# Issuing the two DMA transposes of q and k back to back on the sync queue of a hybrid attention decoder layer

## The chip, the cores and the metric

The kernel runs on 1 core of one Trainium2 chip. The metric is the time of one execution on the device in microseconds (us), the median of several runs. The engines are named as in the profile: PE is TensorE, DVE is VectorE, ACT is ScalarE, POOL is GpSimd, and SP is SyncE, whose queue (SPq) issues nearly all the DMAs.

## The reference

One decoder layer on 256 tokens of width 2048, in float32:

```
h    = rmsnorm(x) ; proj = h @ w_in               # 2048 -> 8192 columns
dq, dk, dv, mq, mk, mv, gate = split(proj)        # 8 "diff" heads, 8 "moba" heads, 128 wide
d_out: per head two softmaxes over 64-wide halves of q and k (causal, ALiBi),
       attn = p0 - lambda * p1 ; rmsnorm(attn @ v) * (1 - 0.2)
m_out: per head causal softmax with ALiBi (with 256 tokens the only block is the own one)
x    = x + (concat(d_out, m_out) * silu(gate)) @ w_out
x    = x + cross attention of rmsnorm(x) (4 heads) into rmsnorm(mem), projected by w_o_mem
out  = rmsnorm(x)
```

## The kernel before

Every float32 matmul with a weight is made of three matmuls on fp32r values: a weight tile w is split into w_hi (an ACT copy, L819) and w_lo = w - w_hi (a DVE subtraction, L1057), the activations likewise, and PE adds hi\*hi, hi\*lo and lo\*hi (L560 to L562). A "half" is 2 x 128 rows by 512 columns of weights, and PE spends 12 matmuls on it. The loads of the raw halves go into a ring of eight buffers (`w_raw`), the split halves into rings of four.

The input projection is cut into 8 pairs of heads, each with 16 halves: halves 0 to 7 make q and k of the pair, halves 8 to 15 make v and gate. The code calls the 16 halves of one pair a window. Pairs 0 to 3 are diff heads, pairs 4 to 7 moba heads. In the window of pair j each engine walks n = 0 to 15, first its share of the splitting for half n + 2 (ACT, DVE) or the matmuls of half n (PE), and then the pieces of attention that are due at n. PE's window j holds the values part of pair j - 1 and the scores of pair j. Since "the pair before" of windows 1 to 4 is a diff pair, those four windows hold the longer chain for y.

The path of q and k of pair a, inside window a:

- n = 8, ACT L847: two copies take q and k (token tiles t = 0 and t = 1) out of PSUM and write them as two planes of 16-bit halves, into `qk_planes` (in the memory of `mems`).
- SP L404 to L409, `turn_qk(a, t)`: waits for the copy of tile t and issues a DMA transpose of 128 x 1024 16-bit values into `qkT_planes`. The profile shows it as DMA_TRANSPOSE at L408.
- POOL L513 to L521, `merge_qk`: for each t it waits until the transpose has landed, and copies the planes back together into `qkT_sb` (L518; in the profile `pool<-mems`).
- n = 12: ACT L852 makes qT_hi and L854 the high part of k; DVE L1103 scales k, and L1109 makes the two low parts.
- n = 13: PE L609 to L617, the scores, which wait for the low parts (`qkT_ready`).

The path of y of the pair before (windows 1 to 4), in the same window: DVE at n = 9, behind the splitting of half 11, runs a chain of fifteen tiny instructions on 128 x 4 values (L1160 to L1171, a reciprocal square root by Newton steps, each waiting for the one before); at n = 10, behind the splitting of half 12, it makes y (L1182 x4). ACT at n = 11 copies y to planes (L896), then splits half 14 (L819), and only then comes to L852. DVE splits half 14 and then comes to L1103. POOL merges the transposed y at L528.

SP's own loop is written by halves too: `load_pair_half` waits until the half that lay in the ring buffer eight halves earlier has been split (`lo_made`) and issues two loads of 256 KB. So SP works on the loads of window j while the other engines are at about n = 8 of window j - 1, and `turns(n, j)` puts the transposes of pair j - 1 behind the loads of half n. All of SP's DMAs leave it in the order of the program. The tail (L451 to L459) does the same for the last pair.

Of the kernel before, what the change touches and what calls it, by code (L numbers as in the profile page):

```python
# [33 lines left out]
NT = SEQ // P  # L34
# [59 lines left out]
X_PARTS = ((0, 256), (256, 512), (512, 1024), (1024, 1536), (1536, 2048))  # L94
WARM_UP = (5, 4, 2)

QK_TURN_AT = (1, 2)
Y_TURN_AT = 4
P_TURN_AT = (10, 11)
MEM_LOAD_AT = 14  # L100
# [26 lines left out]
def program(nc, x, mem, norm_mix_g, w_in, lambda_q1, lambda_k1, lambda_q2, lambda_k2,  # L127
            subln_g, w_out, norm_mem_g, mem_norm_g, w_q_mem, w_kv_mem, w_o_mem, final_g, out):
    with ExitStack() as ctx:
# [249 lines left out]
        def _(sp):  # L379
# [17 lines left out]
            def turn_probabilities(a, u):  # L397

                sp.wait_ge(planes_ready, 2 * a + u + 1)
                sp.nop(nofuse=True)  # L400
                sp.dma_start_transpose(probT_planes[:, u].rearrange("p (i q) -> p i q", q=P), prob_planes[:, u]
                                       ).then_inc(planes_turned[u], 16)

            def turn_qk(a, t):  # L404

                sp.wait_ge(qk_planes_ready, 2 * a + t + 1)
                sp.nop(nofuse=True)
                sp.dma_start_transpose(qkT_planes[:, t].rearrange("p (i q) -> p i q", q=P), qk_planes[:, t]  # L408
                                       ).then_inc(qk_turned[t], 16)  # L409

            def turn_y(a):

                sp.wait_ge(y_planes_ready, a + 1)
                sp.nop(nofuse=True)
                sp.dma_start_transpose(yT_planes.rearrange("p t c -> p (t c)").rearrange("p (i q) -> p i q", q=P),
                                       y_planes.rearrange("p t c -> p (t c)")).then_inc(y_turned, 16)

            def turns(n, j, y_too=True):

                if n in QK_TURN_AT:  # L420
                    turn_qk(j - 1, n - QK_TURN_AT[0])
                if n == Y_TURN_AT and y_too:
                    turn_y(j - 2)
                if n in P_TURN_AT:
                    turn_probabilities(j - 1, n - P_TURN_AT[0])
# [14 lines left out]
            for n in range(PAIR_HALVES):  # L440
                load_pair_half(DIFF, 1, 1, n)
                turns(n, 1, False)
            with sp.Fori(2, KIND_PAIRS) as j:
                for n in range(PAIR_HALVES):
                    load_pair_half(DIFF, j, j, n)
                    turns(n, j)
            with sp.Fori(KIND_PAIRS, PAIRS) as j:
                for n in range(PAIR_HALVES):
                    load_pair_half(MOBA, j, j - KIND_PAIRS, n)
                    turns(n, j)  # L450
# [955 lines left out]
```

## Time and profile before

| | us |
|---|---|
| median of 3 runs | 589.99 (589.55 to 590.5) |
| the profiled execution, its own time | 590.55 |
| its span, first to last instruction | 588.4 |

| engine | busy us | share of the span |
|---|---|---|
| PE (matmuls) | 574.3 | 98% |
| DVE | 434.6 | 74% |
| ACT | 338.5 | 58% |
| POOL | 75.5 | 13% |

The mean granted clock of TensorE is 0.994 of its 2.4 GHz level. 16 DMA engines were busy for 66.4% of the span with SP's queue. A row of a timeline gives the start and the length of an instruction or of a run of them (x2 is two in a row), and in brackets how long its engine sat idle before it and what ended that. A row of the waits gives an engine and line, who it waited for, the sum in us, the number of times and the longest.

### The profile page before, as it was taken

Reading aid. Unit: us, or ns where it says so; the run is one execution under the profiler, and the core shown is the slowest. Engines: PE = TensorE matmul, PEld = TensorE weight load, DVE = VectorE, ACT = ScalarE, POOL = GpSimd, SP = SyncE. Lnnn points to the kernel's source line nnn. Section 1 sums busy time; section 2 is a strip of 40 time slices with the busy share of each in tenths; the row PEclk is TensorE's granted clock in tenths of the full one; section 3 lists DMA queues with packets and bytes.
Section 4 is the critical chain, followed back from the end, with each engine's and each line's share of the span. In section 5 each row is a group of like instructions: output and inputs, shape, how many; then the busy total and the mean of one; then the engine's idle time right before and its main releaser. Section 6 shows DMA issues by size and latency. Waiting matters only on the chain.

```text
span 588.4 us, 8726 instructions
## 1 busy us (share of the span) xinstructions
PE 574.3 (98%) x2738; PEld 479.1 (81%) x2738; DVE 434.6 (74%) x693; ACT 338.5 (58%) x564; POOL 75.5 (13%) x87
## 2 busy tenths in 40 slices
PE   8999999999999999999999999999999999999994
PEld 7878887887888788788888888888888888888883
DVE  4688769888987988886866866957576656755875
ACT  5765754864664774665664664673466665445723
POOL 2010202203111211221310420310000000000000
PEclk9999999999999999999999999999999999999997
DMA  8996766777577677787776874978555555554303
GB/s 276 317 311 215 207 181 180 208 210 202 175 227 188 202 217 188 223 240 194 217 225 168 241 221 146 265 206 320 180 177 155 186 187 189 176 184 144 107 1 143
DMA packets 128349, 117.68 MB, mean 200 GB/s; under 512 B 44050, under 2 KB 110147, under 8 KB 127811
## 3 DMA queue, kind: packets, MB, share of 16 engines
q1 hardware_dynamic: 128290, 117.36, 66.4%
q8 instruction: 13, 0.21, 0.1%
q14 instruction: 14, 0.11, 0.1%
q10 hardware_dynamic: 32, 0.01, 0.0%
HBM read 106.06 MB, written 2.10 MB: 184 GB/s over the span
## 4 chain that ended last, share of the span: by engine, by line
PE 85%; DVE 6%; issue 4%; ACT 4%; ACTq 0%; POOL 0%; DVEq 0%; POOLq 0%
PE ps L560 24%; PE ps L562 24%; PE ps L561 24%; PE ps L591 2%; PE ps L627 2%; ACT w_hi L819 2%; PE ps L609 1%; PE ps L783 1%; PE ps L788 1%; PE ps L784 1%; PE ps L570 1%; DVE pool L1182 1%; DVE w_lo L1057 1%; DVE kT_parts L1109 1%; ACT mems L847 1%
## 5 line engine op out<-in xcount | busy, mean ns | idle before, releaser
L1057 DVE TENSOR_TENSOR w_lo<-w_raw,w_hi 128x1024 fp32r<-128x1024 f32 x187 | 242.6, 1300 | 102.6 <-ACT w_hi L819 100.3
L819 ACT ACTIVATE w_hi<-w_raw 128x1024 fp32r<-128x1024 f32 x187 | 196.1, 1059 | 111.5 <-PE ps L562 109.3
L560 PE MATMUL ps<-w_hi,aT 128*128 128x512 f32 x576 | 226.7, 394 | 0.0
L562 PE MATMUL ps<-w_hi,aT 128*128 128x512 f32 x576 | 224.3, 389 | 0.0
L561 PE MATMUL ps<-w_lo,aT 128*128 128x512 f32 x576 | 224.3, 389 | 0.0
L562 PEld LDWEIGHTS ps<-w_hi,aT 128*128 128x128 f32 x576 | 108.1, 188 | 22.8
L560 PEld LDWEIGHTS ps<-w_hi,aT 128*128 128x128 f32 x576 | 108.2, 188 | 22.5 <-issue 0.4
L561 PEld LDWEIGHTS ps<-w_lo,aT 128*128 128x128 f32 x576 | 108.2, 188 | 21.6
L560 PE MATMUL ps<-w_hi,yT_hi 128*128 128x512 f32 x128 | 50.5, 395 | 0.0
L562 PE MATMUL ps<-w_hi,yT_lo 128*128 128x512 f32 x128 | 49.9, 390 | 0.0
L561 PE MATMUL ps<-w_lo,yT_hi 128*128 128x512 f32 x128 | 49.8, 389 | 0.0
L518 POOL COPY pool<-mems 128x1024 uint16<-128x1024 uint16 x16 | 24.2, 1514 | 166.8 <-DMA mems<-mems 166.8
L864 ACT ACTIVATE pool<-pool,small 128x256 f32<-128x256 f32 (+1 forms) x48 | 21.3, 446 | 21.3 <-DVE small L1129 21.3
L1094 DVE RECIPROCAL pool<-pool 128x128 f32<-128x128 f32 x32 | 30.5, 953 | 1.1
L562 PEld LDWEIGHTS ps<-w_hi,yT_lo 128*128 128x128 f32 x128 | 24.0, 188 | 5.0
L561 PEld LDWEIGHTS ps<-w_lo,yT_hi 128*128 128x128 f32 x128 | 24.1, 188 | 4.8
L560 PEld LDWEIGHTS ps<-w_hi,yT_hi 128*128 128x128 f32 x128 | 24.0, 188 | 4.7
L847 ACT ACTIVATE mems<-ps 128x1024 uint16<-128x1024 uint16 x16 | 15.5, 1020 | 18.5 <-PE ps L562 18.5
L509 POOL COPY probT<-mems 128x768 uint16<-128x768 uint16 x16 | 18.2, 1140 | 59.8 <-DMA mems<-mems 59.8
L1067 DVE SCALAR_TENSOR_TENSOR aT<-ps,gainsT,aT 128x256 fp32r<-128x256 f32 x32 | 14.0, 478 | 13.5 <-ACT aT L829 13.5
L502 POOL TENSOR_TENSOR alibi<-dist,slopes 128x256 f32<-128x256 f32 x16 | 15.5, 987 | 58.6 <-DVE small L1129 58.5
L829 ACT ACTIVATE aT<-ps,gainsT 128x256 fp32r<-128x256 f32 x32 | 13.4, 473 | 14.1 <-PE ps L591 14.1
(166 smaller groups left out, 537.4 us busy)
## 6 DMA issues: line engine op xcount, KB each, us to landing
w_raw<-in_w_in SPq DMA_DIRECT2D x256, 256.0 KB, 3.1
w_raw<-in_w_out SPq DMA_DIRECT2D x64, 256.0 KB, 3.6
w_raw<-in_w_kv_mem SPq DMA_DIRECT2D x32, 256.0 KB, 2.9
w_raw<-in_w_q_mem SPq DMA_DIRECT2D x16, 256.0 KB, 2.9
w_raw<-in_w_o_mem SPq DMA_DIRECT2D x16, 256.0 KB, 3.4
mems<-in_mem SPq DMA_DIRECT2D x1, 2048.0 KB, 9.7
xs<-in_x SPq DMA_DIRECT2D x3, 512.0 KB, 8.3
w_raw<-in_final_g SPq DMA_DIRECT2D x1, 1024.0 KB, 4.6
```

The source lines that it names most:

```text
L502: pool_e.tensor_tensor(alibi[:, u], dist[:, :], slope, ALU.mult).then_inc(alibi_ready, 1)
L509: pool_e.tensor_copy(probT[:, u].rearrange("p i q -> p (i q)").bitcast(U16) .rearrange("p (c h) -> p h c", h=2), probT_planes[:, u].rearra ...
L518: pool_e.tensor_copy(qkT_sb[:, :, t * P:(t + 1) * P].bitcast(U16) .rearrange("p i (q h) -> p h i q", h=2), qkT_planes[:, t].rearrange("p ( ...
L560: pe.matmul(acc, hi[:, k0 + k, tok], w_hi[:, slot, k], start=first and k == 0, stop=False)
L561: pe.matmul(acc, hi[:, k0 + k, tok], w_lo[:, slot, k], start=False, stop=False)
L562: m = pe.matmul(acc, lo[:, k0 + k, tok], w_hi[:, slot, k], start=False, stop=last and k == GK // 2 - 1)
L819: act.activation(w_hi[:, i % SPLITS], raw, ACT.Copy).then_inc(hi_made, 1)
L847: act.activation(qk_planes[:, t].rearrange("p (h c) -> p h c", h=2), ps[:, t, :].bitcast(U16).rearrange("p (c h) -> p h c", h=2), ACT.Copy ...
L864: m = act.activation(prob_sb[:, u, c, cols], prob_sb[:, u, c, cols], ACT.Exp, bias=neg_max[:, u, t, c:c + 1], accum_out=exp_sum[:, c, u, t ...
L1057: dve.tensor_tensor(lo, w_raw[:, i % RAW], hi.bitcast(F32), ALU.subtract).then_inc(lo_made, 1)
L1067: m = dve.scalar_tensor_tensor(lo, ps[:, bank + i, (k % 2) * SEQ:(k % 2 + 1) * SEQ], gainsT[:, gain:gain + 1], hi.bitcast(F32), ALU.mult, ...
L1094: dve.reciprocal(s, s).then_inc(silu_steps, 1)
```

## The change

`QK_TURN_AT` was the pair (1, 2): the transpose of token tile 0 was issued behind the loads of half 1, that of tile 1 behind the loads of half 2. Now both are issued behind the loads of half 1, tile 0 first, and the loads of half 2 follow them. The same holds for the loop of window 1, for the two loops over j and for the tail. No other engine's program is touched, and no instruction is added or removed.

```diff
-QK_TURN_AT = (1, 2)
+QK_TURN_AT = 1
 ...
             def turns(n, j, y_too=True):
 
-                if n in QK_TURN_AT:
-                    turn_qk(j - 1, n - QK_TURN_AT[0])
+                if n == QK_TURN_AT:
+                    for t in range(NT):
+                        turn_qk(j - 1, t)
```

## Rows read from the trace of the kernel before

**Rows 1.** The page, part 1: busy us, share of the span, instructions.
```profile
PE 574.3 (98%) x2738; PEld 479.1 (81%) x2738; DVE 434.6 (74%) x693; ACT 338.5 (58%) x564; POOL 75.5 (13%) x87
```
**Rows 2.** The waits of the whole run: sum us, times, longest.
```profile
ACT qT_hi L852 <- POOL pool L518: 1.6, 4, 0.6
PE ps L609 <- DVE kT_parts L1109: 3.1, 4, 0.8
```
**Rows 3.** ACT's splitting by line: busy, mean ns, then idle before and releasers.
```profile
L819 ACT ACTIVATE w_hi<-w_raw 128x1024 fp32r<-128x1024 f32 x187 | 196.1, 1059 | 111.5 <-PE ps L562 109.3 <-DMA w_raw<-in_w_in 2.0
```
**Rows 4.** The waits of ACT within the first 33 us.
```profile
ACT w_hi L819 <- DMA w_raw<-in_w_in: 2.0, 2, 1.6
```
**Rows 5.** Timeline of window 2, SP's queue: start, length, instruction.
```profile
129.62 1.26 SPq L408 DMA_TRANSPOSE mems<-mems  x1
131.14 0.94 SPq L389 DMA_DIRECT2D w_raw<-in_w_in  x2
132.25 1.23 SPq L408 DMA_TRANSPOSE mems<-mems  x1
133.72 6.31 SPq L389 DMA_DIRECT2D w_raw<-in_w_in  x4
```
**Rows 6.** Timeline of window 2, ACT.
```profile
128.53 1.94 ACT L847 ACTIVATE mems<-ps 128x1024 uint16<-128x1024 uint16 x2 [1.99 <-PE ps L562]
...
140.01 1.06 ACT L896 ACTIVATE mems<-pool 128x1024 uint16<-128x1024 uint16 x1 [4.99 <-DVE pool L1182]
...
141.93 0.62 ACT L852 ACTIVATE qT_hi<-pool 128x512 fp32r<-128x512 f32 x1
```
**Rows 7.** Timeline of window 2, POOL: the two merges of q and k.
```profile
132.83 1.34 POOL L518 COPY pool<-mems 128x1024 uint16<-128x1024 uint16 x1 [14.45 <-DMA mems<-mems]
136.58 1.35 POOL L518 COPY pool<-mems 128x1024 uint16<-128x1024 uint16 x1 [2.41 <-DMA mems<-mems]
```
**Rows 8.** Timeline of window 2, DVE: parts of the Newton chain, splitting, y, k.
```profile
132.99 1.14 DVE L1164 SCALAR_TENSOR_TENSOR small<-small 128x4 f32<-128x4 f32 x1
134.16 0.17 DVE L1167 TENSOR_SCALAR small<-small 128x4 f32<-128x4 f32 x1
134.37 0.17 DVE L1076 TENSOR_SCALAR small<-small 128x4 int32<-128x4 int32 x1
134.57 0.16 DVE L1080 SCALAR_TENSOR_TENSOR small<-small 128x4 f32<-128x4 f32 x1
...
136.63 2.31 DVE L1057 TENSOR_TENSOR w_lo<-w_raw,w_hi 128x1024 fp32r<-128x1024 f32 x1
138.87 1.11 DVE L1182 SCALAR_TENSOR_TENSOR pool<-ps,small,pool 128x128 f32<-128x128 f32 x4
...
144.59 1.01 DVE L1109 TENSOR_TENSOR kT_parts<-pool,kT_parts 128x512 fp32r<-128x512 f32 x1
```
**Rows 9.** Timeline of PE: the scores of window 2, and of window 5.
```profile
145.65 0.50 PE L609 MATMUL ps<-kT_parts,qT_hi 64*128 64x256 f32 x4 [0.81 <-DVE kT_parts L1109]
...
286.49 0.40 PE L609 MATMUL ps<-kT_parts,qT_hi 128*128 128x256 f32 x2
```
**Rows 10.** Line L1057 over the run: min/median/max ns, first and last start.
```profile
L1057 DVE TENSOR_TENSOR w_lo<-w_raw,w_hi x187: 1206/1225/2315, 9.9 to 560.1; 128x1024 fp32r<-128x1024 f32 x187
```
**Rows 11.** Timeline of DVE: the splitting of half 12 in windows 1, 3, 4.
```profile
89.44 2.14 DVE L1057 TENSOR_TENSOR w_lo<-w_raw,w_hi 128x1024 fp32r<-128x1024 f32 x1
...
184.16 2.17 DVE L1057 TENSOR_TENSOR w_lo<-w_raw,w_hi 128x1024 fp32r<-128x1024 f32 x1
...
231.26 2.20 DVE L1057 TENSOR_TENSOR w_lo<-w_raw,w_hi 128x1024 fp32r<-128x1024 f32 x1
```
**Rows 12.** Line L1164 over the run: min/median/max ns.
```profile
L1164 DVE SCALAR_TENSOR_TENSOR small<-small x4: 161/1136/1153, 85.8 to 227.7; 128x4 f32<-128x4 f32 x4
```
**Rows 13.** Timeline of POOL near 257 us: a merge of probabilities.
```profile
256.60 2.05 POOL L509 COPY probT<-mems 128x768 uint16<-128x768 uint16 x1 [1.82 <-DMA mems<-mems]
```
**Rows 14.** Timeline of DVE near 257 us: a tensor_scalar twice.
```profile
257.65 1.08 DVE L1092 TENSOR_SCALAR pool<-pool 128x128 f32<-128x128 f32 x1
...
261.10 0.22 DVE L1092 TENSOR_SCALAR pool<-pool 128x128 f32<-128x128 f32 x1
```

## The prediction

> **What bounds the kernel now.** I read the page first. PE is busy for 574.3 of 588.4 us [rows 1], so whatever an edit of the DMA order does, it can only change PE's idle time, 14 us in all, most of it at the two ends. Next I read the waits, for the places where the path of q and k could hold PE up. There is one: PE stands at L609 for 3.1 us in four windows [rows 2]. These are windows 1 to 4; the one of window 2 is 0.81 us [rows 9]. In window 5 PE comes to the same line with no idle time [rows 9]. So a reader's question is what ends last in front of L609 in windows 1 to 4, and the timelines of one such window on SP, ACT, POOL and DVE answer it.
>
> In window 2 ACT finishes the two planes of q and k at 130.47 [rows 6], SP issues the turns at 129.62 and 132.25 with two loads between them [rows 5], and POOL merges them at 132.83 to 134.17 and 136.58 to 137.93 [rows 7]. The merged q and k are read by ACT L852 only at 141.93 [rows 6]: the second merge is 4.0 us early. L852 is late for another reason: ACT sat idle for 4.99 us before L896 [rows 6], waiting for DVE's y (L1182, 138.87 to 139.98) [rows 8]; then come L896, one splitting and L852, each right behind the other. DVE's k part ends at 145.60 [rows 8], PE starts at 145.65 [rows 9]. The last thing in front of L609 is therefore the chain Newton steps, splitting of half 12, y, L896, L852, k. A microsecond more or less in that chain is one in PE's wait, as long as 0.8 us are not used up.
>
> Then I compared POOL's and DVE's rows, since these touch that chain. L1164 works on 4 elements per partition, and takes 1.14 us while POOL's first merge runs; it ends at 134.13, POOL at 134.17 [rows 7, 8]. Its neighbours of the same size take 0.16 to 0.17 [rows 8]. The splitting of half 12 begins 0.05 us after the second merge and takes 2.31 us against a median of 1.225 [rows 7, 8, 10]. So each merge stops the DVE instruction that starts behind it until the copy is over, and both stops lie in the chain that PE waits for. This pattern stands in all four windows: 2.14, 2.17 and 2.20 in the other three [rows 11]; L1164 has it in three of them, with a median of 1.136 [rows 12], and in the fourth it is the instruction ahead of it.
>
> **The change part by part.** It removes nothing and adds nothing; it moves one transpose per pair ahead of two loads.
>
> *The loads of half 2* go from 131.14 to about 1.49 us later (a turn of 1.23 and the gap of 0.26 that stands between 130.88 and 131.14) [rows 5], and the loads of half 3 then start at 133.6 to 133.7, where they start now. Each load fills a buffer that is used eight halves later, some 21 us. ACT waited for a load for 2.0 us in the whole run [rows 3], all of it in the first 33 us [rows 4], ahead of the first moved turn. Cost nothing; the cover is some 15 us deep.
>
> *The wait of the second turn* now stands ahead of the loads of half 2. It is for the second plane, ready at 130.47, before the first turn has left SP at 130.88 [rows 5, 6]. Cost nothing.
>
> *The second merge.* A turn takes 3.21 us from issue to the start of its merge (129.62 to 132.83), and the second, behind 512 KB of loads, 4.33 (132.25 to 136.58) [rows 5, 7]. The trace shows no two turns back to back. By the first row it lands at 131.14 + 3.21 = 134.35; by the other at 135.5. I take 134.35, since then too nothing stands between it and an idle queue but a turn that has already been sent. The merge starts 0.18 us behind the end of the first instead of 2.41 us.
>
> This earlier merge gains nothing on the path of q and k, by the 4.0 us above. In windows 5 to 7 and 0 ACT does wait for it, 1.6 us in all [rows 2], but PE has no idle time there [rows 9]. Worth nothing.
>
> *What the merge stops on DVE.* Removed: the stop of the splitting of half 12, 2.14 + 2.31 + 2.17 + 2.20 - 4 x 1.225 = 3.92 us over four windows. Added: a copy of 1.35 us that starts at 134.35, in the middle of the Newton chain, which now runs undisturbed from 134.16 to 136.5. Which step it stops isn't shown for this size. If a tensor_scalar is stopped too, it is L1076 at 134.37 [rows 8]: it ends at about 134.35 + 1.35 - 0.04 = 135.66 instead of 134.54, 1.12 us. If only the instructions with two inputs are stopped, it is L1080 at 134.57, ending at 135.66 instead of 134.73, 0.93 us, and up to 0.2 less in a window where two tensor_scalars are still ahead. The four windows run in nearly the same phase, so the sums are 4.48 and 3.5 to 3.7. The nearest row for a tensor_scalar is L1092 at 257.65, 1.08 us instead of 0.22 while a POOL copy ran to 258.65 [rows 13, 14]; it is wider (128 instead of 4), but the same operation. I take the first: 4.48 - 3.92 = +0.56 us; the other end is -0.3.
>
> What the rows show here has a rule: the Trainium skill, SBUF — State Buffer, section "Who interferes with whom", says that DVE and GpSimd share a pair of ports as an exclusive lock, held for the whole instruction, that DVE instructions with two SBUF inputs contend with a GpSimd instruction that reads SBUF, and that a tensor_scalar can when it runs in a two-port mode. L1164 (two inputs, 1.14) and L1092 (1.08) agree. By that rule the time would be the +0.56 of the sum if the 4-wide steps run in such a mode, and -0.3 if they don't; no row here shows which.
>
> *The end of window and the rest.* Behind the chain everything (L896, turn of y, L852, k) keeps its distances. The profiled execution would go from a span of 588.4 to about 589.0. Its own time was 590.55, 0.56 above the median of the three runs, so I add the difference to the median: 589.99 + 0.56 = 590.5.
>
> **The rivals.**
>
> 1. *Only two-input steps are stopped*: the same story with the other end of the price, -0.3, 589.7. For it: it needs no assumption about 4-wide tensor_scalars; against it: L1092.
> 2. *The second turn lands as late as it does now*, or somewhere in the chain's second half, for instance since two transposes are served one after the other. Then the stop falls on another step of the same chain, or again on the splitting: 590.0 to 590.4. For it: no row shows two turns in a row. Against it: nothing much.
> 3. *Slower: POOL doesn't give the port back between the merges.* The second copy needs only to have landed within the first, that is 1.34 us after it instead of my 1.52. SP's spacing could be 1.26 plus a gap of 0.1 rather than 0.26 [rows 5]. If POOL then goes first, L1164 waits for two copies. Each window loses 1.35 + some 0.1 and gets back 0.98 (3.92 / 4): +0.47, four times, +1.9 us, 591.9. Against it: in the rows DVE's stopped instruction ended 0.04 us before POOL's record, so it seems to be the next in line; and my estimate leaves 0.18 us.
> 4. *Faster: the merge is what L609 waits for after all.* Then up to the whole 3.1 us [rows 2] come back, 586.9. Against it the 4.0 us between the merge and L852 [rows 6, 7].
>
> **How the numbers follow.** Forecast 590.5: 0.42; rival 1, 0.28; rival 2, 0.18; rival 3, 0.09; rival 4, 0.03. The runs before spread over 0.95 us, so about 0.2% (1.2 us, that is 588.8 and 591.2) is what a measurement can tell from no change. Forecast and rivals 1 and 2 lie inside it; a little of each leaks over the edge by scatter. Faster 0.05, same 0.84, slower 0.11. The range goes from rival 1 less 0.6 of scatter to just under rival 3: 589.1 to 591.6.
>
> **What would show it right or wrong.** In the profile after: the turns of a pair 1.5 us apart on SP and the loads of half 2 behind them; the second merge 1.5 us behind the first instead of 3.75; the splitting of half 12 back at 1.2 us in windows 1 to 4; in its place a second step of the Newton chain at 1.1 to 1.3 us, a tensor_scalar (L1167 or L1076) for the forecast, L1080 to L1084 for rival 1; ACT no longer waiting for POOL at L852; PE's wait at L609 still in four windows with 3.5 us instead of 3.1 (2.8 for rival 1, 4.9 for rival 3, none for rival 4). Everything else within 0.1 us. I would be wrong if ACT began to wait for loads, if the turns slowed each other beyond 136.6, or if the moved merge met an instruction in windows 5 to 7 that PE waits for.

## The result: 0.22% slower, with both of VectorE's stops now in the Newton chain

| | before | after |
|---|---|---|
| median of 20 runs, same job | 589.83 | 591.10 |
| lowest and highest | 588.49, 591.11 | 590.90, 591.58 |
| ratio, 95% interval | | 1.0022, 1.0015 to 1.0029 |
| the profiled execution, its own time | 590.55 | 591.33 |
| its span | 588.4 | 589.2 |

All times are in us. A job is a set of runs made together. The time went up by 1.27 at the median, but only by 0.78 between the two profiled executions. In the changed kernel the lines of the file from L421 on are one higher: L1057 of before is L1058 of after, L1076 is L1077, L1167 is L1168.

The first thing to look at is window 2 again. On SP's queue the two turns are now in a row, and six loads follow, where rows 5 had turn, loads, turn, loads:

```profile
130.07 2.69 SPq L408 DMA_TRANSPOSE mems<-mems  x2
133.00 7.66 SPq L389 DMA_DIRECT2D w_raw<-in_w_in  x6
```

POOL's two merges (rows 7: 132.83 and 136.58) are in a row too, 2.68 us for two copies of 1.34:

```profile
133.54 2.68 POOL L519 COPY pool<-mems 128x1024 uint16<-128x1024 uint16 x2 [14.69 <-DMA mems<-mems]
```

And this is DVE's timeline across them (answering rows 8), from the Newton chain to y:

```profile
133.44 0.16 DVE L1165 SCALAR_TENSOR_TENSOR small<-small 128x4 f32<-128x4 f32 x1
133.63 1.29 DVE L1168 TENSOR_SCALAR small<-small 128x4 f32<-128x4 f32 x1
134.96 1.29 DVE L1077 TENSOR_SCALAR small<-small 128x4 int32<-128x4 int32 x1
136.28 0.16 DVE L1081 SCALAR_TENSOR_TENSOR small<-small 128x4 f32<-128x4 f32 x1
...
138.34 1.23 DVE L1058 TENSOR_TENSOR w_lo<-w_raw,w_hi 128x1024 fp32r<-128x1024 f32 x1
139.48 1.12 DVE L1183 SCALAR_TENSOR_TENSOR pool<-ps,small,pool 128x128 f32<-128x128 f32 x4
```

Two tensor_scalars of 4 elements per partition, 0.17 us each when nothing else runs (rows 8), take 1.29 us each, one per copy. The splitting of half 12 is back from 2.31 to 1.23 us. So each window has two stopped DVE instructions, as before; one of the two has moved from the splitting into the Newton chain. PE's wait at the scores (rows 9: 0.81) is

```profile
146.27 0.51 PE L610 MATMUL ps<-kT_parts,qT_hi 64*128 64x256 f32 x4 [0.91 <-DVE kT_parts L1110]
```

and over the run (rows 2), with ACT's waits for loads (rows 3, 4) and for the merge:

```profile
PE ps L610 <- DVE kT_parts L1110: 3.6, 4, 0.9
ACT w_hi L820 <- DMA w_raw<-in_w_in: 1.7, 2, 1.5
ACT qT_hi L853 <- POOL pool L519: 1.0, 1, 1.0
```

So PE waits 3.6 us instead of 3.1, in the same four windows. The two tensor_scalars repeat in each of them: L1168 takes 1.21 to 1.29 us, L1077 1.24 to 1.33. ACT waits no more for loads than it did, and for the merge once, in window 0, where PE has no idle time. The scores of window 4 begin 0.76 us later than in the profile of before, those of window 7 0.80, and the span is 0.8 longer: 0.11 of it was there at the scores of window 0 already, and 0.65 arises from there to the scores of window 4.

### The profile page after: what moved, and what is told of

It reads as the page before. It is cut to its first block, busy times and chain, and to the rows that moved or that the text cites. A ratio compares the mean times of both kernels' runs of the same rounds, so it can differ in the third digit from the quotient of the medians.

```text
span 589.2 us, 8726 instructions
## 1 busy us (share of the span) xinstructions
PE 574.2 (97%) x2738; PEld 478.4 (81%) x2738; DVE 432.9 (73%) x693; ACT 338.7 (57%) x564; POOL 76.7 (13%) x87
## 4 chain that ended last, share of the span: by engine, by line
PE 81%; DVE 7%; issue 4%; ACT 3%; SPq 3%; DMA 2%; ACTq 0%; DVEq 0%
PE ps L561 24%; PE ps L563 23%; PE ps L562 23%; PE ps L628 2%; ACT w_hi L820 2%; DMA w_raw<-in_w_in 2%; SPq L389 1%; PE ps L610 1%; PE ps L785 1%; PE ps L784 1%; PE ps L789 1%; PE ps L592 1%; DVE small L1077 1%; DVE small L1168 1%; DVE pool L1183 1%
## 5 line engine op out<-in xcount | busy, mean ns | idle before, releaser
L1058 DVE TENSOR_TENSOR w_lo<-w_raw,w_hi 128x1024 fp32r<-128x1024 f32 x187 | 235.4, 1262 | 105.1 <-ACT w_hi L820 103.1
L519 POOL COPY pool<-mems 128x1024 uint16<-128x1024 uint16 x16 | 28.0, 1779 | 152.0 <-DMA mems<-mems 152.0
```

The lines of the kernel that those rows point to most:

```text
L519: pool_e.tensor_copy(qkT_sb[:, :, t * P:(t + 1) * P].bitcast(U16) .rearrange("p i (q h) -> p h i q", h=2), qkT_planes[:, t].rearrange("p ( ...
L1058: dve.tensor_tensor(lo, w_raw[:, i % RAW], hi.bitcast(F32), ALU.subtract).then_inc(lo_made, 1)
```

## The experiments

The theory: each POOL merge stops one DVE instruction for the length of the copy; if that instruction is in the chain to y, PE pays. The rivals: that the order on the DMA queue costs something itself, and that an early merge is what counts. A second question was why the medians differ by more than the profiles.

### Both kernels once more (e1, e2)

No edit. 

> The kernel before, unchanged, timed and profiled once more. Theory (race): in the first profile the second merge of q and k on POOL started within 0.25 us of the DVE's splitting of half 12 in each of windows 1 to 4, and DVE was stopped four times out of four; whoever is first holds the port. In another execution DVE should be first in some windows: the splitting then takes 1.2 us instead of 2.1 to 2.3, the copy is stopped instead, and PE's wait at the scores of that window falls from 0.8 to 0 to 0.2 us. Expected here: median 589.8, runs spread over 2 us, at least one window of the profile won by DVE. Rival (the spread has nothing to do with the merges): all four windows as in the first profile, whatever the time of the execution.

> The changed kernel, unchanged. Theory (race): both copies start in the middle of the Newton chain, where DVE is always stopped twice, so there is nothing left to win: median 591.1, spread below 0.7 us, and the profile again shows L1168 and L1077 at 1.2 to 1.3 us in all four windows. Rival: the spread is as wide as that of the kernel before.

On this chip the 23 runs of the kernel before that stand beside e1 to e4 took 590.53 (588.65 to 590.93); e1, 12 more runs of the same kernel, took 590.29 (588.73 to 590.75), ratio 0.9996 (0.9987 to 1.0005). The changed kernel took 591.04 (590.90 to 591.61), ratio 1.0013 (1.0005 to 1.0022). The half of the expectation about the spread holds: 0.7 us against over 2. The race did not show: the profile of e1 (590.18) has four stops in four windows. But it showed that the second merge isn't tied to its place. It starts 3.20 to 3.88 us behind the first, and in windows 1 and 4 it stopped a step at the end of the Newton chain (L1084, 1.18 us, and L1171, 1.23 us) instead of the splitting. In e2 L1168 and L1077 take 1.21 to 1.33 us in all four windows, as expected.

### The second merge held back until y is made (e3, e4)

```diff
                 for t in range(NT):
+                    if t == 1 and not isinstance(a, int):
+                        pool_e.wait_ge(y_ready, a)
                     pool_e.wait_ge(qk_turned[t], 16 * a + 16)
```

e3 has this in the kernel before, e4 in the changed one.

> The order of turns of the kernel before; the second merge of q and k on POOL waits in addition until DVE has made y of that window (y_ready), from pair 1 on. Theory (the port stop in the chain of y is the whole price): the splitting of half 12 takes 1.2 us always, y comes 1.0 us earlier, PE's wait at the scores falls from 0.8 to under 0.2 us in windows 1 to 4, and the time is 587.3 to 588.0. Rival (the merge is needed early by ACT or PE): ACT waits for the late merge, PE's wait stays or grows, 590 or more.

> The order of turns of the changed kernel, with the same gate as the run before. Theory (the moved loads and the two turns in a row cost nothing, only the place of the second copy does): the same time as with the order of before, within 0.3 us, 587.3 to 588.0. Rival (the order on the DMA queue has a cost of its own, from the loads of half 2 that come later or from turns that slow each other): about 1.3 us slower than the gated kernel with the order of before.

Measured: 586.91 (ratio 0.9946, 0.9934 to 0.9958) and 587.00 (0.9947, 0.9935 to 0.9959). That is 0.3 to 0.4 us below the lower end of what the theory expected, and the two are equal within 0.1. With the gate the second merge has the same place in both, and the first still stops one step of the Newton chain in each, so the two kernels differ in the order on the DMA queue and in little else, and no difference is left to see. The rival of the queue, which had 1.3 us, falls. In window 2 of e3 the splitting of half 12 is free, and the merge is the one that is stopped, 2.19 us, while DVE splits half 13:

```profile
138.17 2.19 POOL L520 COPY pool<-mems 128x1024 uint16<-128x1024 uint16 x1 [4.89 <-DVE pool L1184]
```
```profile
135.75 1.23 DVE L1059 TENSOR_TENSOR w_lo<-w_raw,w_hi 128x1024 fp32r<-128x1024 f32 x1
136.90 1.12 DVE L1184 SCALAR_TENSOR_TENSOR pool<-ps,small,pool 128x128 f32<-128x128 f32 x4
137.94 1.21 DVE L1059 TENSOR_TENSOR w_lo<-w_raw,w_hi 128x1024 fp32r<-128x1024 f32 x1
```

PE's row of waits at the scores is gone from e3 and e4 altogether. From the scores of window 2 to those of window 3 PE is now busy for all of 46.45 us, where it had been 46.59 busy and 0.80 idle. So a window gives back its wait and some 0.1 us of recorded matmul time besides, which is how 3.1 us of waits became 3.6 of time, and PE leaves nothing more to win there.

### The opposite of the change (e5)

```diff
-QK_TURN_AT = (1, 2)
+QK_TURN_AT = (1, 3)
 ...
-                    turn_qk(j - 1, n - QK_TURN_AT[0])
+                    turn_qk(j - 1, QK_TURN_AT.index(n))
```

> The opposite of the change: the second turn goes behind the loads of half 3 instead of half 2. No wait is added. Theory (the place of the second copy is all that counts): SP issues it some 1.5 us later than before, it lands at about the start of y or behind it, the splitting of half 12 is not stopped, PE's waits of windows 1 to 4 are gone, and the time is that of the gated kernels, 586.8 to 587.6, with a spread below 0.7 us. Rival (the earlier the transposes are, the better; or it was the gate itself that helped): 590 or more.

586.82 (586.81 to 587.22), ratio 0.9947 (0.9933 to 0.9960). With no wait added, a turn issued later gives 3.4 us, about as much as the gate. In window 2 the second merge starts at 138.21, behind y, and it is now late for ACT, which waits 0.34 us for it at L852 there, 10.7 us in six windows over the run. PE doesn't notice:

```profile
138.21 2.10 POOL L518 COPY pool<-mems 128x1024 uint16<-128x1024 uint16 x1 [4.98 <-DMA mems<-mems]
```
```profile
ACT qT_hi L852 <- POOL pool L518: 10.7, 6, 2.6
```

This answers "the earlier the better": here the merge is later, ACT waits over six times as long as in the kernel before (1.6, rows 2), and the kernel is faster by 0.5%. It also shows that a stop costs by its place. In windows 1 and 3 POOL was first again, and the splitting of half 13, behind y, was stopped. Two splittings take 3.39 us here, with one stopped, and PE had no wait in these windows either:

```profile
91.11 1.37 POOL L518 COPY pool<-mems 128x1024 uint16<-128x1024 uint16 x1 [4.33 <-DMA mems<-mems]
```
```profile
91.42 3.39 DVE L1057 TENSOR_TENSOR w_lo<-w_raw,w_hi 128x1024 fp32r<-128x1024 f32 x2
```

### A third copy behind the two (e6)

```diff
                                        ).then_inc(qk_merged, 1)
+                pool_e.tensor_copy(spare.rearrange("p (r c) -> p r c", r=2),
+                                   dist[:, :].bitcast(U16).unsqueeze(1).to_broadcast([P, 2, 2 * SEQ]))
```

> The changed kernel with a third copy on POOL behind the second merge of each pair, of 1024 16-bit values from dist into a tile that nobody reads (extra work; the result is the reference's). Theory (each POOL copy behind the other stops one more instruction of the Newton chain for its whole length, and PE waits for the chain): L1081 or its neighbour takes 1.1 to 1.3 us as well, PE's waits grow by 1.1 to 1.2 us in each of four windows, 591.1 + 4.4 to 4.9 = 595.5 to 596.0. Rival (what matters is when the merge is ready, or DVE loses only the first stop): 591.1 to 592, since nobody waits for the third copy.

594.15 (594.09 to 594.50), 3.05 above the 591.10 that the changed kernel took in the job of the result, where 4.4 to 4.9 were expected. The mechanism is as expected, and the size is off since this copy is shorter. POOL and DVE in window 2:

```profile
134.37 2.73 POOL L520 COPY pool<-mems 128x1024 uint16<-128x1024 uint16 x2 [14.73 <-DMA mems<-mems]
137.00 1.04 POOL L524 COPY spare<-dist 128x1024 uint16<-128x1024 uint16 x1
```
```profile
134.38 1.29 DVE L1168 SCALAR_TENSOR_TENSOR small<-small 128x4 f32<-128x4 f32 x1
135.70 0.17 DVE L1171 TENSOR_SCALAR small<-small 128x4 f32<-128x4 f32 x1
135.91 1.21 DVE L1080 TENSOR_SCALAR small<-small 128x4 int32<-128x4 int32 x1
137.15 0.91 DVE L1084 SCALAR_TENSOR_TENSOR small<-small 128x4 f32<-128x4 f32 x1
```

A copy of 1.04 us stops L1084 for 0.91 - 0.16 = 0.75 us. The other three windows have 0.75, 0.75 and 0.74 at the same line, together 3.0, and 3.05 were measured. Nobody waits for this copy; it costs only by what it stops. PE's wait at the scores is 3.6, as in the changed kernel, and a second one has come up, since half 12 is split too late for its matmuls:

```profile
PE ps L564 <- DVE w_lo L1061: 1.9, 4, 0.5
```

That is 1.9 of the 3 us. Most of the rest lies in PE's busy time, which is 0.16 to 0.28 us higher from one window's scores to the next than in the changed kernel (46.79 against 46.51 in the last of them).

### Both merges held back (e7)

The same gate for both token tiles (`if not isinstance(a, int):`), in the kernel before.

> The order of turns of the kernel before, and both merges of q and k on POOL wait until DVE has made y. Theory (PE's waits in windows 1 to 4 were all that there was to win, and one stop less wins them whole): the Newton chain is not stopped at all and y comes another 1.0 us earlier, but PE has nothing left to wait for, so 586.9 again, within 0.3 us; or up to 1 us more if the two merges, now in a row behind y, hold L852 up. Rival (each stop has its price, 0.8 to 1 us per window): 583 to 584.

589.76 (589.55 to 589.99), ratio 0.9996 (0.9987 to 1.0005). A miss: 1.9 us above the upper end that the theory gave, though far from the rival's 583. In window 2 no step of the chain is stopped, and y is done 39.6 us behind the scores of window 1 instead of 41.7, but now the merges are the last to come:

```profile
137.93 4.36 POOL L520 COPY pool<-mems 128x1024 uint16<-128x1024 uint16 x2 [20.43 <-DVE pool L1184]
```
```profile
138.71 1.05 ACT L821 ACTIVATE w_hi<-w_raw 128x1024 fp32r<-128x1024 f32 x1
142.31 0.63 ACT L854 ACTIVATE qT_hi<-pool 128x512 fp32r<-128x512 f32 x1 [2.56 <-POOL pool L520]
```

The two copies take 4.36 us instead of 2.7, since DVE's splittings stop them in turn, ACT waits 2.56 us, and PE 0.63 us in this window and 2.4 in all four. So a merge can be too late as well: here there is room for one behind y, not for two. The rival's 583 to 584 did not come. e7 alone doesn't price the first merge's stop, since the late merges cost PE time of their own; but e3 had left PE no idle time in these windows that a second freed stop could give back.

### Half a microsecond (e9) and four more profiles of the kernel before (e8, e10 to e12)

```diff
                     pool_e.nop(nofuse=True)
+                    if t == 1:
+                        for c in range(12):
+                            pool_e.memset(spare[:, c:c + 1], 0.0)
```

> The kernel before, with twelve memsets of one column of an unused tile on POOL between the landing of the second turn and the second merge, some 0.04 us each by the memsets at the start of the trace: the merge starts about 0.5 us later and nothing else changes. In three profiles of the kernel before it started 0.05 to 0.7 us ahead of the splitting of half 12. Theory (a race for the port, decided by tenths of a us): now DVE is first in all or nearly all four windows, the splitting takes 1.2 us, the merge is stopped (2.0 to 2.5 us), PE's waits go, and the median is 586.8 to 587.8. Rival (a merge that comes half a microsecond later is half a microsecond worse or the same): 590 to 591.

586.74 (586.52 to 587.69), ratio 0.9949 (0.9935 to 0.9962). Half a microsecond of work that nobody needs makes the kernel 3.5 us faster. In window 2:

```profile
135.61 0.55 POOL L521 MEMSET spare<- 128x1 f32 x12 [2.09 <-DMA mems<-mems]
136.10 2.33 POOL L522 COPY pool<-mems 128x1024 uint16<-128x1024 uint16 x1
```
```profile
135.71 0.16 DVE L1175 TENSOR_TENSOR small<-small 128x4 f32<-128x4 f32 x1
135.99 1.23 DVE L1061 TENSOR_TENSOR w_lo<-w_raw,w_hi 128x1024 fp32r<-128x1024 f32 x1
137.14 1.12 DVE L1186 SCALAR_TENSOR_TENSOR pool<-ps,small,pool 128x128 f32<-128x128 f32 x4
```

DVE was first by 0.11 us, and now the copy takes 2.33 us and the splitting 1.23. In rows 7 and 8 POOL was first by 0.05 us, with 1.35 and 2.31. This is the same pair of instructions, with the price on the other side. The memsets themselves stopped nothing: L1175 ran beside them in its usual 0.16 us.

> The kernel before once more, for a third profile. In two profiles the second merge started 0.05 to 0.3 us before or behind the end of the Newton chain and always stopped a DVE instruction (of the chain or the splitting of half 12). Theory (race): if the execution is one near 589 us, at least one window shows the splitting at 1.2 us, no stopped step late in the chain, and a second merge that is itself stopped (about 2.2 us); an execution near 590.5 us shows none. Rival: the time varies without that.

> The kernel before, one more profile, to meet one of its faster executions (its times run from 588.5 to 591.1). Theory (race): if this one is below 589.5 us, at least one window shows the splitting of half 12 at 1.2 us with no late step of the Newton chain stopped, and PE's wait there is near 0. Rival: a fast execution with four stops.

> As the look before it: below 589.5 us with at least one window won by DVE (theory), or with none (rival).

> As the two looks before it: below 589.5 us with at least one window won by DVE (theory), or with none (rival).

These four executions took 590.34, 590.23, 590.74 and 590.22. None was below 589.5, so the question asked of them stays unanswered. With the first profile and e1 they are six profiles with 24 windows 1 to 4. The second merge started 3.20 to 3.88 us behind the first, and in all 24 windows it stopped a DVE instruction: the splitting of half 12, or L1084 or L1171 at the end of the Newton chain. In window 2 of e12 it was L1171:

```profile
136.05 1.34 POOL L518 COPY pool<-mems 128x1024 uint16<-128x1024 uint16 x1 [2.10 <-DMA mems<-mems]
```
```profile
136.13 1.23 DVE L1171 TENSOR_TENSOR small<-small 128x4 f32<-128x4 f32 x1
137.48 1.23 DVE L1057 TENSOR_TENSOR w_lo<-w_raw,w_hi 128x1024 fp32r<-128x1024 f32 x1
```

## Why the prediction was right, and where it wasn't

**What bounds the kernel.** Held. e3, e4, e5 and e9 took the stop of the second merge out of the chain to y in three ways, and PE's waits at the scores went with it, 3.4 to 3.6 us of time for 3.1 us of waits; the rest is the 0.1 us of busy time per window read in e3.

**The loads and the wait of the second turn: cost nothing.** Held: ACT waits 1.7 us for loads (2.0 before), and e3 and e4 agree within 0.1 us.

**The second merge: ready early, worth nothing.** Held, and e5 shows it from the other side.

**When the merges come.** Two misses of 0.3 and 0.2 us. The first merge had been left where it was, but it starts 3.47 us behind its issue (130.07 to 133.54) instead of 3.21. In the sixteen windows where another turn comes right behind it in the queue (after, e2, e4, e6) it is 3.36 to 3.50, in all others (e7 aside, whose first merge waits for y) 3.15 to 3.23. So its copy now stops L1168 and not a step ahead of it. The second was put at 1.52 us behind the first, but it was ready by the end of the first copy, 1.34. That was the point from which rival 3 was to decide. Yet POOL didn't keep DVE out for two copies: the stopped L1168 got in between them and the next one, L1077, was stopped. Rival 3 had the condition right and the consequence wrong. So each copy stops one instruction, and by e6 a third copy a third one.

**Which step is stopped.** The forecast took tensor_scalars as stopped, by one wide row (rows 14), against rival 1. The profile after has exactly that: L1168 and L1077, in all four windows, and so has that of e2. The second of them is L1076 of before, the step that the forecast named. What the Trainium skill says in SBUF — State Buffer, section "Who interferes with whom", of a port pair held for the whole instruction agrees with both sides seen here: DVE at 1.29 us instead of 0.17, and POOL at 2.33 instead of 1.35, by who came first.

**The sum.** By the first profiles, the stops of the four windows make 8.8 us after (2.18, 2.24, 2.17, 2.20, each duration less 0.17) and 8.0 before (3.92, and 4.08 for the first merge: 0.97, 0.98, 1.14, 0.99). That is +0.8 instead of +0.56. The second merge's stops are 4.48 for 3.92, exactly as forecast; the rest is the first merge, which stops its instruction for 1.04 to 1.12 us now, 4.31 in all, a term that the sum had at nothing. ACT was to wait no more for POOL at L852; it did once, 1.0 us in window 0, and not at all in e2. PE's waits grew by 0.5, the scores of window 4 came 0.65 later beyond the 0.11 of the start, and the profiled execution 0.78.

**The step that failed** is the last one: "so I add the difference to the median". The difference was between profiled executions, and the profile of before was one in which all four windows were stopped. Added to that execution's own 590.55 it would have given 591.11. Nearly all times of the kernel before lie in three groups, 590.2 to 590.9, 589.1 to 589.8, and 588.5 to 588.9, whose middles are 0.8 to 1.0 us apart, about what one window without its stop would save (PE's wait there is 0.7 to 0.9 us, and e3's windows are 0.9 shorter). In the job of the result half of the runs lay below 589.7, in the job of e1 2 of 23 and 2 of e1's own 12. Against the upper group, near 590.5, the change costs 0.5 to 0.6 us, as forecast (591.04 against 590.53 in e1's job); the rest of the 1.27 is in the runs of the lower groups, which the changed kernel hasn't got. The likely reading is that before sometimes had a window or two without a stop in the chain, and after never has. For it: with nothing but a gate on the second merge e3's six runs lie within 0.4 us, so the spread goes with the time of that merge. e9 shows that tenths of a us decide it, and its own times (586.5 to 586.7, and 587.4, 587.7) look like one window lost now and then. That the lower groups are windows won by DVE is still inferred and not shown; no execution from them was profiled.

So 591.10 lies inside the range of 589.1 to 591.6 and 0.6 above the forecast: the mechanism of the forecast is the one seen, and the baseline was half a microsecond too low. With 0.22% it is just beyond the 0.2% that the text had drawn between the same and slower, and slower had been given 0.11; the interval (0.15% to 0.29%) holds that bound.

## What to carry to other kernels

Moving a transfer forward also moves the work that its landing releases, and in this kernel a POOL copy and a DVE instruction kept each other out for their whole length: before issuing anything earlier, see what DVE is doing at the new time and who waits for it. A copy that is needed 4 us later is best put where the other engine is off the critical chain: here one turn behind the loads of half 3 instead of half 2, which costs no instruction, gave 586.8 against 590.3, faster than both kernels. And before adding a difference read from two profiles to a median, look at the spread of the times; where a kernel's runs differ by 2 us and its neighbour's by 0.7, look for a race.

## What the runs showed of the hardware

- POOL copies and DVE instructions with two SBUF inputs, or tensor_scalars down to 4 elements per partition (float32 and int32), keep each other out for a whole instruction. Behind a copy of 1.34, tensor_scalars of 0.17 us took 1.21 to 1.33 (after, e2, e4), two-input steps of 0.16 took 1.13 to 1.30, and the splitting of 1.23 took 2.12 to 2.31 (the six profiles of before). Behind DVE's splitting a copy of 1.35 took 1.69 to 2.33 and ended 1.2 us after the splitting each time (e3, e4, e5, e9). Being first by 0.05 or 0.11 us decides.
- Memsets on POOL stopped none of these steps: L1175, with two inputs, kept its 0.16 us beside them (e9, window 2).
- y (L1186 in e9; its wide inputs are one in PSUM and one in SBUF) took its usual 1.12 us in e9 although the held-up copy ran beside it.
- Two waiting copies in a row don't lock DVE out: one stopped instruction passes between them (after, e2, and e6 with three copies).
- Two DMA transposes of 256 KB issued some 1.4 us apart (2.69 us for the two, 1.25 for one): the merge of the first began 3.4 to 3.5 us behind its issue instead of 3.2, that of the second could have begun 3.4 us behind or less, instead of 3.8 to 4.4 with two loads between.
